# The roots of five norms: sums of ready squares first, and visits of modulation behind the transposes

## The reference, cut to what matters

```python
def rms_norm(x, w):
    xf = x.astype(jnp.float32)
    y = xf * lax.rsqrt(jnp.mean(xf * xf, axis=-1, keepdims=True) + NORM_EPS)
    return (y * w.astype(jnp.float32)).astype(x.dtype)

def adaln_params(cond, w_mod, b_mod):
    m = jax.nn.silu(cond) @ w_mod + b_mod
    return jnp.split(m[..., None, :], N_MOD, axis=-1)

def modulate(h, shift, scale):
    return h * (1 + scale) + shift
```

## Time and profile before

| | |
|---|---|
| runs | 2065.0, 2065.08, 2071.91 us, median 2065.08 us |
| profiled execution | 2065.3 us |
| its span, first to last instruction | 2063.6 us |
| TensorE busy | 2043.2 us, 99% of the span |
| VectorE busy | 1365.1 us, 66% |
| ScalarE busy | 1100.2 us, 53% |
| mean granted clock of TensorE | 0.997 |

### The profile page before, as it was taken

The page is one execution under the profiler, slowest core; times in us unless marked ns, Lnnn a source line. Parts: engine busy times, 40 slices in busy tenths (PEclk is TensorE's granted clock), DMA queues, the critical chain, the costliest instruction groups (busy, mean ns, idle before and its releaser), DMA issues.

```text
span 2063.6 us, 36368 instructions
## 1 busy us (share of the span) xinstructions
PE 2043.2 (99%) x14742; PEld 1827.8 (89%) x14742; DVE 1365.1 (66%) x2356; ACT 1100.2 (53%) x1839; POOL 68.7 (3%) x55
## 2 busy tenths in 40 slices
PE   9999999999999999999999999999999999999998
PEld 9999999999999999997677887778788888999998
DVE  6687767567787786574565345665555667668786
ACT  5576685545676785453475233433332347645554
POOL 2210000000300000000000000000000000000000
PEclk9999999999999999999999999999999999999999
DMA  7556545566656535563223434433333343454552
GB/s 285 181 162 211 188 144 183 185 222 229 227 177 194 194 124 200 199 243 136 84 72 113 143 133 173 143 115 131 113 133 133 112 158 116 148 174 164 185 179 78
DMA packets 97351, 334.43 MB, mean 162 GB/s; under 512 B 11552, under 2 KB 16160, under 8 KB 96928
## 3 DMA queue, kind: packets, MB, share of 16 engines
q1 hardware_dynamic: 97184, 332.10, 47.4%
HBM read 326.94 MB, written 1.18 MB: 159 GB/s over the span
## 4 chain that ended last, share of the span: by engine, by line
PE 92%; DVE 4%; ACT 2%; issue 1%; DVEq 0%; ACTq 0%
PE ps L961 25%; PE ps L962 25%; PE ps L963 24%; PE ps L1044 2%; PE ps L974 2%; PE ps L975 2%; PE ps L976 2%; DVE t_lo L1686 1%; PE ps L1261 1%; ACT t_hi L1356 1%; PE ps L1117 1%; PE ps L1271 1%; PE ps L1282 1%; PE ps L983 1%; PE ps L1133 1%
## 5 line engine op out<-in xcount | busy, mean ns | idle before, releaser
L961 PE MATMUL ps<-t_RB,t_hi 128*128 128x256 f32 (+1 forms) x3712 | 1160.8, 313 | 4.0 <-ACT t_MT L1402 1.4
L962 PE MATMUL ps<-t_RB,t_hi 128*128 128x256 f32 (+1 forms) x3712 | 1144.4, 308 | 0.0
L963 PE MATMUL ps<-t_RB,t_lo 128*128 128x256 f32 (+1 forms) x3712 | 1144.0, 308 | 0.0
L1686 DVE TENSOR_TENSOR t_lo<-t_raw,t_hi 128x1024 fp32r<-128x1024 f32 (+1 forms) x503 | 610.7, 1229 | 363.4 <-ACT t_hi L1356 362.1
L961 PEld LDWEIGHTS ps<-t_RB,t_hi 128*128 128x128 f32 x3712 | 707.9, 191 | 73.5 <-issue 23.1
L963 PEld LDWEIGHTS ps<-t_RB,t_lo 128*128 128x128 f32 x3712 | 708.2, 191 | 35.3
L962 PEld LDWEIGHTS ps<-t_RB,t_hi 128*128 128x128 f32 x3712 | 708.4, 191 | 33.0
L1356 ACT ACTIVATE t_hi<-t_raw 128x1024 fp32r<-128x1024 f32 (+1 forms) x506 | 519.4, 1041 | 371.7 <-PE ps L963 349.4
L2126 DVE SCALAR_TENSOR_TENSOR t_A<-ps,t_V,t_A 128x510 f32<-128x510 f32 (+1 forms) x176 | 102.1, 611 | 89.0 <-ACT t_A L1646 87.4
L1646 ACT ACTIVATE t_A<-ps,t_V 128x512 f32<-128x512 f32 (+1 forms) x88 | 48.4, 576 | 127.0 <-PE ps L963 127.0
L2099 DVE SCALAR_TENSOR_TENSOR t_X<-ps,t_MOD,t_X 128x256 f32<-128x256 f32 x168 | 72.6, 477 | 32.9 <-PE ps L963 32.9
(11 more groups left out here) (308 smaller groups left out, 1869.9 us busy)
## 6 DMA issues: line engine op xcount, KB each, us to landing
t_raw<-in_W SPq DMA_DIRECT2D x586, 512.0 KB, 3.9
t_A<-cu_scratch SPq DMA_DIRECT2D x8, 512.0 KB, 6.1
t_B<-cu_scratch SPq DMA_DIRECT2D x8, 512.0 KB, 5.8
t_raw<-in_W SPq DMA_DIRECT2D x16, 256.0 KB, 3.2
t_A<-in_C SPq DMA_DIRECT2D x2, 1536.0 KB, 6.6
t_A<-t_T SPq DMA_DIRECT2D x40, 64.0 KB, 4.4
t_A<-t_T SPq DMA_DIRECT2D x40, 32.0 KB, 1.9
t_X<-in_X SPq DMA_DIRECT2D x2, 512.0 KB, 4.3
```

The costliest lines, as they stand in the source:

```text
L961: mm(o, hi[:, w], xh(k), start=k == 0 and j == 0, stop=False)
L962: mm(o, hi[:, w], xl(k), start=False, stop=False)
L963: i = mm(o, lo[:, w], xh(k), start=False, stop=k == nkt - 1 and m == u.x[1] - 1)
L1686: tt(t.lo[s][:, 0:w], t.raw[r][:, 0:w], t.hi[s][:, 0:w].bitcast(F), ALU.subtract).then_inc(*up("dve", ("split", u.i)))
```

## The change

A new unit `rstda` sums the ready squares, and comes first in the root of norms 1 to 7; the sum of the last squares follows when they are there, into the same bank. Visits are placed anew: one between the two sums, one behind them, two behind the transposes (`(1, 1, 2)`; norm 2 `(1, 1, 0)`, norm 3 `(0, 1, 0)`). Visits that stand together share a bank (they are summed in it), and a unit `modsum` empties it once; that of the visits behind the transposes comes after the norm. The last GEMM ahead of a root puts the early half on ScalarE ahead of the last square (`high_first`), and VectorE makes its low half right behind the last tile (`lows`). 19 of the dummies go. In the second half of the kernel eight visits are kept back for norms 5 and 6 (`keep`), so that norm 6 has four, where it had none, and norm 5 four, where it had three; norm 1 has four as before, norms 2 and 3 three together, where they had five, norm 4 four as before.

```diff
+    def high_first(self):
+
+        if self.late:
+            self.low.append(self.late.pop(0) + NS)
+            self.add("split", i=self.low[-1], x=("low",))
+
+    def lows(self):
+        while self.low:
+            self.add("low", i=self.low.pop(0))
+
     def late_splits(self):
         while self.late:
             self.early_split()
 
     def mod_turn(self):
         self.turn += 1
-        if self.every and self.turn % self.every == 0:
+        if self.every and self.turn % self.every == 0 and len(self.mods) > self.keep:
             self.some_mods(1)
 
     def some_mods(self, n):
 
         for _ in range(n):
-            if self.mods:
-                l, c = self.mods.pop(0)
-                if c % 4 == 0 and len(self.open) == 2:
-                    self.turn_mod()
-                self.add("mod", l=l, c=c, g=(self.bank(),))
-                if c % 4 == 3:
-                    self.open.append((l, c // 4, 0))
+            self.mod_sums(self.visits(1))
+
+    def visits(self, n):
+        out = []
+        self.more_visits(out, n)
+        return out
+
+    def more_visits(self, out, n):
+
+        for l, c in self.mods[:n]:
+            first = not out or c % 4 == 0
+            if c % 4 == 0 and len(self.open) == 2:
+                self.turn_mod()
+            g = (self.bank(),) if first else out[-1].g
+            self.add("mod", l=l, c=c, g=g, s=(first, False))
+            out.append(self.units[-1])
+        del self.mods[:n]
+
+    def mod_sums(self, out):
+
+        for u, after in zip(out, out[1:] + [None]):
+            if after is None or after.s[0]:
+                u.s = (u.s[0], True)
+                first = max(v.c for v in out if v.s[0] and v.c <= u.c and v.l == u.l)
+                self.add("modsum", l=u.l, c=u.c, g=u.g, x=(first,))
+                if u.c % 4 == 3:
+                    self.open.append((u.l, u.c // 4, 0))
 
```

The places at which visits stand, the table of dummies, and the parts of TensorE and of the engine that empties a bank:

```diff
             if last and urgent:
+                self.late += [i + h for h in range(-(-self.width[i] // HF))]
+                self.high_first()
                 self.drain()
-                self.late += [i + h for h in range(-(-self.width[i] // HF))]
             if (self.fine or urgent) and not last:
...
     def layer1(self, l):
-        b = self.rstd(l, (2, 1, 1) if l else (0, 0, 0))
+        b = self.rstd(l, (1, 1, 2) if l else (0, 0, 0))
...
 
-        self.some_mods(fill[0])
-        self.add("rstd", l=t, g=(self.bank(),), n=self.sums[t])
-        self.some_mods(fill[1])
+        g = (self.bank(),)
+        if t:
+            self.add("rstda", l=t, g=g, n=self.sums[t])
+        self.lows()
+        ahead = self.visits(fill[0])
+        self.add("rstd", l=t, g=g, n=self.sums[t])
+        self.more_visits(ahead, fill[1])
+        self.mod_sums(ahead)
         b = (self.bank(),)
         self.add("rstdb", l=t, g=b)
-        self.some_mods(fill[2])
+        self.behind = self.visits(fill[2])
         return b
 
+    def behind_sums(self):
+        self.mod_sums(self.behind)
+        self.behind = []
+
     def plain(self, t):
-        b = self.rstd(t, (2, 1, 0))
+        b = self.rstd(t, (0, 0, 0))
         for k in range(0, 8, 2):
             self.add("plain", l=t, c=k, g=b)
...
-            self.early_split()
-            b = self.rstd(t, (2, 1, 1))
+            b = self.rstd(t, (1, 1, 2))
             self.add("norm2", l=t, g=b, x=range(8))
+            self.behind_sums()
...
-            self.early_split()
-        b = self.rstd(t + 1, (2, 1, 1))
+        b = self.rstd(t + 1, (1, 1, 2))
         self.add("norm2", l=t + 1, g=b, x=range(8))
+        self.behind_sums()
         self.late_splits()
-        self.every = 0 if last else 3
+        self.every, self.keep = 0 if last else 3, 8
 
...
-IDLE = {0: (11, 2, 5), 1: (0, 0, 4), 4: (0, 0, 4), 5: (0, 0, 5), 6: (2, 3, 4)}
+IDLE = {0: (11, 2, 5), 1: (0, 0, 1), 4: (0, 0, 1), 5: (0, 0, 1), 6: (0, 0, 0)}
...
         (n, z0), s, one = blocks_of(u.l), u.l, t.ones[:, 0:1]
-        q.wait_ge(at("c1") if s else at("c32"))
+        if s == 0:
+            q.wait_ge(at("c32"))
+            b = bank(u)
+            idle(b, s, 0)
+            q.wait_ge(at("c1"), at("sqadd", 0, 7))
+            src, o = t.S0[1], 0
+        elif s == 8:
+            b, src, o = bank(u), t.SQA, z0
+            q.wait_ge(at("c1"), at("sqadd", 8, 7))
+        else:
+            b, src, o = t.gb[u.g[0] % 4], t.NT[:, 512:512 + n * 128], 0
+            idle(b, s, 0)
+            q.wait_ge(at("sqa", s, 7))
+        for z in range(n):
+            i = mm(b[:, z:z + 1], src[:, (o + z) * 128:(o + z) * 128 + 128], one, start=s in (0, 8) and z == 0, stop=z == n - 1)
+        i.then_inc(*up("pe", ("ssq", s), *([("nt", *u.n[1])] if 0 < s < 8 else [])))
+
+    def rstda(u):
+
+        (n, z0), one = blocks_of(u.l), t.ones[:, 0:1]
         b = bank(u)
-        idle(b, s, 0)
-        q.wait_ge(at("c1"))
-        if s == 0:
-            parts = [(("sqadd", 0, 7), t.S0[1], 0)]
-        else:
-            h = t.NT[:, 512:512 + n * 128]
-            parts = [(("sqadd", s, 7 if s == 8 else 6), t.SQA, z0)] + ([(("sqa", s, 7), h, 0)] if s < 8 else [])
-        for p, (point, src, o) in enumerate(parts):
-            q.wait_ge(at(*point))
-            for z in range(n):
-                i = mm(b[:, z:z + 1], src[:, (o + z) * 128:(o + z) * 128 + 128], one, start=p == 0 and z == 0,
-                       stop=p == len(parts) - 1 and z == n - 1)
-        i.then_inc(*up("pe", ("ssq", s), *([("nt", *u.n[1])] if 0 < s < 8 else [])))
+        q.wait_ge(at("sqadd", u.l, 6))
+        for z in range(n):
+            mm(b[:, z:z + 1], t.SQA[:, (z0 + z) * 128:(z0 + z) * 128 + 128], one, start=z == 0, stop=False)
 
     def rstdb(u):
...
             for c in range(4):
-                i = mm(b[32 * c:32 * c + 32, 0:256], t.C32[:, k, :], t.raw[r % NR][:, c * 256:c * 256 + 256], start=h == 0,
-                       stop=h == 1)
+                i = mm(b[32 * c:32 * c + 32, 0:256], t.C32[:, k, :], t.raw[r % NR][:, c * 256:c * 256 + 256],
+                       start=u.s[0] and h == 0, stop=u.s[1] and h == 1)
             i.then_inc(*up("pe", ("modmm", u.l, u.c, h)))
...
 
-    def mod(u):
+    def modsum(u):
         l, (j, r) = u.l, divmod(u.c, 4)
-        if r == 0:
+        if u.x[0] % 4 == 0:
             q.wait_ge(was("modt", *mod_before(l, j, 2)), at("modmm", l, u.c, 1))
...
+
+    def low_half(u):
+        s, r, w = u.i % NS, u.x[1] % NR, u.x[0]
+        q.wait_ge(at("hi", u.i))
+        tt(t.lo[s][:, 0:w], t.raw[r][:, 0:w], t.hi[s][:, 0:w].bitcast(F), ALU.subtract).then_inc(*up("dve", ("split", u.i)))
```

More of the change, by code:

```diff
@@ L171, in __init__ @@
         self.mods, self.open = [(l, c) for l in range(L) for c in range(24)], []
-        self.width, self.late, self.sums = {}, [], {}
+        self.width, self.late, self.sums, self.keep, self.low = {}, [], {}, 0, []
     def add(self, kind, **k):
@@ L611, in block2 @@
         self.add("s1", l=l, x=(4, t + 1))
-        if last:
-            self.early_split()
-        b = self.rstd(t + 1, (2, 1, 1))
+        b = self.rstd(t + 1, (1, 1, 2))
         self.add("norm2", l=t + 1, g=b, x=range(8))
+        self.behind_sums()
         self.late_splits()
-        self.every = 0 if last else 3
+        self.every, self.keep = 0 if last else 3, 8
         def down(g):
@@ L673, in between @@
         chunks = [self.uf_chunk(0, c) for c in range(2)]
-        self.early_split()
-        b = self.rstd(2, (2, 1, 0))
+        b = self.rstd(2, (1, 1, 0))
         squares = self.squares(3)
@@ L680, in between @@
         self.uf(0, 0, chunks[0], 1, False)
-        self.some_mods(1)
         b = self.rstd(3, (0, 1, 0))
@@ L1306, in tensor @@
     half_of = {(u.l, u.c): u.n[0] for u in units if u.kind == "z" and u.x[2] == 0}
-    todo = dict(rstd=rstd, rstdb=rstdb, mod=mod, mod2=mod2, q=of_h, k=of_h, conv=of_h, rope=of_h, z=of_h, gate=lambda u: of_h(u, ("gatemm", u.l)),
+    todo = dict(rstda=rstda, rstd=rstd, rstdb=rstdb, mod=mod, mod2=mod2, q=of_h, k=of_h, conv=of_h, rope=of_h, z=of_h, gate=lambda u: of_h(u, ("gatemm", u.l)),
                 wide=wide, small4=small4, vc=vc, vb=vc, scores=scores, turn=turn, pv=pv, ssm0=ssm0, ssm3=ssm3, ssm4=ssm4,
@@ L1658, in glu @@
             act(t.Y2[:, yi, 0:tw], V, ACT.Copy).then_inc(*up("act", ("gluh", l, pr, m), ("glu", l, g, yi), ("fr", l, 0, pr, m)))
-    todo = dict(split=split, sq=sq, rstd=rstd, cond=cond, norm1=norm1, mod=mod, q=qk, k=qk, vc=vproj, vb=vproj, conv=conv, conv2=conv2,
+    todo = dict(split=split, sq=sq, rstd=rstd, cond=cond, norm1=norm1, modsum=modsum, q=qk, k=qk, vc=vproj, vb=vproj, conv=conv, conv2=conv2,
                 small1=small1, small2=small2, exp=exp, turn=turn, pv=pv, ssm0=ssm0, ssm1=ssm1, ssm1b=ssm1b, ssm1c=ssm1c, ssm3=ssm3, z=z, zsq=zsq, ysplit=ysplit,
@@ L1735, in plain, with modsum @@
                 *up("dve", ("x", s + 1, k), ("gfree", u.g[0])))
-    def mod(u):
+    def modsum(u):
         l, (j, r) = u.l, divmod(u.c, 4)
-        if r:
+        if u.x[0] % 4:
```

(12 more changed lines are left out.)

## The result

The changed kernel takes 2070.16 us (median of 20 runs, 2067.11 to 2075.9) against 2065.16 (20 runs, 2063.88 to 2071.91): a ratio of 1.0023, with a 95% interval of 1.0016 to 1.003. It is slower by 5 us where 3.8 us of gain were forecast, and outside the range. The profiled execution took 2068.9, 3.6 more than that of before.

What follows compares the result with a forecast made beforehand. TensorE, busy 99% of the span, was taken as the bound. Root, stream and stall terms of −6.1 plus +2.3 for the clock gave −3.8 us: 2061.5 profiled, 2061.3 median, range 2056 to 2066.5.

Steps and rivals of the forecast that it cites:

- norm 4: Root of norm 4: the GEMM's start moves with the norm, late rows costing little, −2.2 us; −0.8 if they cost more.
- Norm 1: Root of norm 1: transposes and norm earlier, but the GEMM waits for the visit's late second row, −0.8 us.
- Norm 6: Root of norm 6: four visits replace nine dummies and the fourth's rows land late, +1.6 us, plus +0.8 for a clock fall.
- norm 5: Root of norm 5: transposes at 1664.6 instead of 1665.46, −0.9 us; its clock fall stays and costs 0.
- Norms 2 and 3: Roots of norms 2 and 3: transposes earlier, −0.6 and −1.1 us; a clock fall behind norm 3 costs +1.5.
- the stall: Feed-forward stage: TensorE waits for VectorE's add of a visit's bank instead of ScalarE's copy, +0.9 us.
- the stream: Between the GEMMs of the feed-forward stage: three fewer visits at 1.0 us each, −3.0 us.
- The clock: Roots: half clock follows waits among visits and sums; new falls behind norms 3 and 6, none behind 1 and 4, +2.3 us.
- Rival B: All five roots: the clock falls behind each because the dummies are gone, +1.4 us, 2066.5; chance 0.10.
- rival C: Roots: waits as short as these don't lower the clock, so −6.1 us alone, 2059.0; chance 0.09.
- A: Norms 1 and 6: the late rows land in time, 2057.3 us; chance 0.15.
- D: GEMMs behind four roots: visits' loads push weight loads back, each GEMM waits for its second half, +5 us, 2066.3; chance 0.10.

## Why the prediction was wrong

**The step that failed** is norm 4: "The GEMM behind follows the norm's pace for its first chunks, so its start moves with the norm and the late rows of the fourth visit cost little". The transposes and the norm came as worked out (1277.19, and the norm at 1277.88 against 1277.7), but the GEMM started at 1286.01. I had gone through the weight halves in SyncE's queue, and not through what else stands in it. The early half's load waits there for the low half (1275.83), and C3, which was issued at 1266.46 before, is held behind it and comes out between the two rows: the second row lands 7.6 after its issue instead of 4.0, TensorE waits 4.71 for it, and norm 4 costs 3.1 instead of giving 2.2. The order of SyncE's queue, of before and of the changed kernel, follows from the two programs alone; before, C3 stood among loads in the same way, but went out 6.6 ahead of the root:

```
L873 DMA t_raw4<-in_W 128x1024
L918 DMA t_A<-in_C3 128x3072
L873 DMA t_raw5<-in_W 128x1024

L911 DMA t_raw1<-in_W 128x1024
L956 DMA t_A<-in_C3 128x3072
L911 DMA t_raw2<-in_W 128x1024
```

Moving C3 alone gives back the 5.0 (2065.16), and norm 4 then gains 0.7 at the GEMM's start and 2.0 further on. So with C3 out of the way the sentence holds, the pair of late rows costs little in norm 4, and the step failed by C3 alone.

**Norm 1**: the mechanism was right and the size off. The rows landed 4.4 and 5.3 after their issue instead of 3.2 and 4.0, so +1.1 instead of −0.8, and a fall of the clock behind the wait that I had placed elsewhere. Over the runs the first row of this pair took 3.4 to 4.4 and the second 4.9 to 6.7, so 4.0 from a pair in norm 5 was too low; the trace of before already had 5.6 for a load issued in norm 1. Why loads take longer there is open. In the run with this visit in norm 2 the GEMM starts 2.4 earlier than before.

**Norm 6** and **norm 5**: in norm 6 +2.0, against +1.6 and +0.8 for a fall that didn't come; the 0.4 more are its rows, which landed 3.4 and 4.4 after their issue instead of 3.2 and 4.0. In norm 5 the transposes stood at 1665.99 instead of 1664.6, as the clock fell on the visits ahead of them (1.93 for one), and the norm cost 0.6 instead of giving 0.9. I had put the price of that fall at 0.

**Norms 2 and 3, the stall, the stream**: the stall came within 0.1 of its term, and norms 2 and 3 within 0.2, but for the fall that didn't come. TensorE waits 1.44 and 1.29 for the ready squares there as forecast; filling these waits brought nothing that can be told. Three visits fewer in the stream gave 4.0, 1.3 each and not 1.0.

**The clock**: the prediction named a fall behind norm 1 or 4 as a sign of being wrong, and both came. Its sentence "So a wait among visits and sums is what goes before a fall here" is too narrow. In the kernel with norm 1's visit in norm 2 the clock is at half right behind the wait of 2.22 for the bank, among GEMM work (first line); behind the same wait the changed kernel has the full clock (second line):

```profile
1359.40:1362.70 3.30, 3.30 (x8) 0.50 0.07 30
1368.60:1371.90 3.30, 3.30 (x14) 1.00 0.08 31
```

Of the nine profiled executions that have this wait, five show a fall behind it and four don't; what decides it is open. Nor does the root stay the same: norms 1, 4 and 5 lost the clock in the changed kernel, norms 3 and 5 with C3 alone, norm 5 alone with the dummies back where no visit is late in norm 1. Rival B priced a fall behind every root at +1.4 in all; this execution shows three. Norm 3, which I had priced at 1.5, shows none. Over the runs of the changed kernel time and clock go together: 2067.11 at a mean clock of 0.996, 2075.9 at 0.992. The rule of the Trainium skill that stood beside rival C (TensorE: Matmul & The Clock Gate, section "Why this matters for your kernels"), a drop only after longer gaps without matmuls, is not borne out: the fall in norm 5 after came behind a wait of 1.17. The fall inside norm 4's wait of 4.71 agrees with it.

**The other rivals**: A did not come, as the late rows landed later than taken and not earlier. D's price isn't in the profile either: the one wait of a GEMM for a low half of weights is 0.9 in all, before and after.
